# RWKV-7 chunk stage of a hybrid decoder step: the bonus products on GpSimd, the second half's new state, four filler matmuls and the first loads take other places

## The reference, cut to what matters

```python
def _wkv_step(S, inp):
    r, w, k, v, a, b = inp
    sa = jnp.einsum('bhvk,bhk->bhv', S, a)
    S = S * w[:, :, None, :] + sa[..., None] * b[:, :, None, :] + v[..., None] * k[:, :, None, :]
    return S, jnp.einsum('bhvk,bhk->bhv', S, r)
...
S_T, y = lax.scan(_wkv_step, wkv0, (tm(r), tm(decay), tm(k), tm(v), tm(-kk), tm(kk * a)))
mean = jnp.mean(y, axis=-1, keepdims=True)
var = jnp.mean(jnp.square(y - mean), axis=-1, keepdims=True)
y = ((y - mean) * lax.rsqrt(var + GN_EPS)).reshape(B, T, D) * ln_w + ln_b
y = y + (jnp.sum(r * k * r_k, axis=-1, keepdims=True) * v).reshape(B, T, D)
out = (y * g) @ w_o
```

## Time and profile before

| | us |
|---|---|
| median of 3 runs | 3388.64 |
| lowest and highest run | 3384.31, 3389.98 |
| the profiled execution's own time | 3387.22 |
| its span in the profile | 3385.5 |
| PE busy | 3241.1 (96%) |
| DVE busy | 1845.6 (55%) |
| ACT busy | 1334.3 (39%) |
| POOL busy | 1204.2 (36%) |

### The profile page before, as it was taken

How to read it: one execution, slowest core, us unless ns; L and a number is a source line. 1 busy time by engine, 2 the same in 40 slices (tenths; PEclk the granted TensorE clock), 3 DMA queues, 4 the chain that set the end, 5 groups by cost and what they waited for, 6 DMA issues and landing times.

```text
span 3385.5 us, 71725 instructions
## 1 busy us (share of the span) xinstructions
PE 3241.1 (96%) x26244; PEld 2942.4 (87%) x26244; DVE 1845.6 (55%) x3138; ACT 1334.3 (39%) x2785; POOL 1204.2 (36%) x842
## 2 busy tenths in 40 slices
PE   8999999999999999999999888988999999999998
PEld 6688887688999999989899777777887899999998
DVE  3566663126444588853332577677731644448885
ACT  2244445413545433313223445555421255543332
POOL 0000000012666777702232122222232076677771
PEclk9999999899999999999999899999969999999999
DMA  3122225401544544331232110001151054454442
GB/s 110 46 77 73 72 61 169 156 1 51 159 160 155 170 141 140 127 100 58 66 109 78 60 36 27 26 27 33 33 183 36 20 160 156 154 171 147 146 145 80
DMA packets 303577, 331.56 MB, mean 98 GB/s; under 512 B 54350, under 2 KB 285825, under 8 KB 303138
## 3 DMA queue, kind: packets, MB, share of 16 engines
q1 hardware_dynamic: 297346, 309.17, 28.6%
q0 software_dynamic: 6048, 19.73, 1.8%
HBM read 232.57 MB, written 116.69 MB: 103 GB/s over the span
## 4 chain that ended last, share of the span: by engine, by line
PE 74%; DVE 9%; PEld 6%; issue 4%; POOL 3%; ACT 2%; DMA 1%; SPq 1%; ACTq 1%; DVEq 0%; PEldq 0%; POOLq 0%
PE bank L631 70%; PEld bank L631 6%; PE bank L639 4%; POOL wloA L2034 1%; DVE arena L3547 1%; POOL arena L2034 1%; DVE arena L3701 1%; SPq L1662 1%; POOL wloS L2034 1%; DVE hT L3618 1%; DVE arena L3118 0%; ACT arena L2255 0%; ACTq L2714 0%; DVE arena L3010 0%; DVE arena L3564 0%
## 5 line engine op out<-in xcount | busy, mean ns | idle before, releaser
L631 PE MATMUL bank<-arena 128*128 128x268 f32 (+18 forms) x7294 | 972.7, 328 | 59.2 <-DVE hT L3618 15.5
L631 PEld LDWEIGHTS bank<-arena 128*128 128x128 f32 (+7 forms) x7294 | 756.5, 174 | 248.7 <-issue 43.1
L2255 ACT COPY arena<-bank 128x512 f32<-128x512 f32 (+15 forms) x523 | 233.4, 483 | 651.6 <-PE bank L631 450.6
L2034 POOL TENSOR_TENSOR arena<-arena 128x512 f32<-128x512 f32 x120 | 165.3, 1378 | 674.9 <-PE bank L631 448.3
L2478 ACT ACTIVATE whiS<-arena 128x512 fp32r<-128x512 f32 x180 | 113.0, 628 | 406.1 <-POOL arena L2034 392.9
L2034 POOL TENSOR_TENSOR wloA<-arena,whiA 128x512 fp32r<-128x512 f32 x180 | 261.6, 1468 | 0.4 <-ACT whiA L2475 0.4
L2034 POOL TENSOR_TENSOR wloS<-arena,whiS 128x512 fp32r<-128x512 f32 x180 | 238.8, 1341 | 49.1 <-ACT whiS L2478 49.1
L3413 DVE TENSOR_TENSOR hT<-hT,bank 128x536 f32<-128x536 f32 x280 | 197.6, 706 | 83.0 <-PE bank L631 82.6
L631 PE MATMUL bank<-hiT,whiS 128*128 128x268 f32 x768 | 199.9, 288 | 7.5 <-DVE loT L3255 3.8
L639 PE MATMUL bank<-table,arena 128*128 128x128 f32 (+5 forms) x1354 | 174.2, 271 | 31.2 <-DVE arena L3130 13.1
L3260 DVE TENSOR_TENSOR arena<-std,bank 128x268 f32<-128x268 f32 x192 | 80.4, 432 | 216.7 <-PE bank L631 208.4
(11 more groups left out here) (321 smaller groups left out, 8630.6 us busy)
## 6 DMA issues: line engine op xcount, KB each, us to landing
u_scratch<-arena SPq DMA_DIRECT2D x480, 134.0 KB, 1.8
arena<-in_ffn_w_up SPq DMA_DIRECT2D x64, 512.0 KB, 4.1
arena<-u_scratch SPq DMA_DIRECT2D x56, 536.0 KB, 5.2
arena<-in_ffn_w_down SPq DMA_DIRECT2D x112, 256.0 KB, 4.0
arena<-u_scratch SPq DMA_DIRECT2D x56, 402.0 KB, 6.0
arena<-past_scratch SPq DMA_DIRECT2D x32, 640.0 KB, 6.9
past_scratch<-in_cache_kv_latent SPq DMA_DIRECT2D x128, 128.0 KB, 2.4
past_scratch<-in_cache_k_rope SPq DMA_DIRECT2D x128, 32.0 KB, 2.1
```

Of the source, the lines that this page charges most:

```text
L631: return pe.matmul(out, lhsT, rhs, start=first, stop=last, skip_group_check=group)
L2034: return pool.tensor_tensor(out, a, b, op)
L2255: lane.do(act.copy(dst, b if view is None else view(b)), ring.drained)
```

## The change

It has four parts.

1. **GpSimd, `chunk`**: the bonus of a chunk is no longer the end of the chunk before. `bonus(c)` opens chunk c for c = 1 to 7, behind a wait for `low_b` (DVE has ended `low_inverses(c)`). The tail's bonus stays at the end of chunk 7. Since SyncE's load of r and k waits for the bonus, it moves too.
2. **DVE, `new_half`** is split. `new_taken` is the mask that frees the bank and stays; `new_summed` is the addition and the product. For the first half both follow each other as before. For the second half `new_summed(1)` moves behind `level_16(0)` of the next chunk, ahead of `scale_state`; in chunk 7 it stays.
3. **TensorE, `chunk`**: in chunk 0, which has no gates, four `keep_busy` matmuls stand where the others have the gates, behind `level_16(c, 1, ...)`.
4. **SyncE**: ahead of chunk 0 the load of r and k of chunk 1 comes first, ahead of the wait for the stores of v and the load of v of chunk 0.

```diff
@@ TensorE, chunk
                 if finish:
                     gates(c - 1, P)
+                else:
+                    for _ in range(4):
+                        keep_busy(ra)
@@ SyncE
+            bonus_b.wait(sp, 0)
+            load_r_k(1)
             for par in range(2):
                 sp.wait_ge(stg_s[par], staged_n)
             load_v(0, 0)
-            bonus_b.wait(sp, 0)
-            load_r_k(1)
             load_v(1, 1)
@@ GpSimd, chunk
+                if finish:
+                    low_b.wait(pool, c)
+                    bonus(c, P)
                 if prepare:
                     scale_keys(c + 1, wn)
...
                 if prepare:
                     decay_r(c + 1, 1 - par, wn)
+                if wn == TAIL:
                     bonus(c + 1, wn)
                 if finish:
                     store_z(c - 1)
@@ DVE
-            def new_half(d):
+            def new_taken():
                 b = ring.bank()
+                lane.do(dve.tensor_tensor(P1.rearrange("p (k w) -> p k w", k=4), b[:, :].rearrange("p (k w) -> p k w", k=4),
+                                          halves.unsqueeze(1).broadcast_to([P, 4, P]), ALU.mult), ring.drained)
+
+            def new_summed(d):
                 cts = slice(4 * d, 4 * d + 4)
                 new = P1.rearrange("p (k w) -> p k w", k=4)
-                lane.do(dve.tensor_tensor(new, b[:, :].rearrange("p (k w) -> p k w", k=4),
-                                          halves.unsqueeze(1).broadcast_to([P, 4, P]), ALU.mult), ring.drained)
                 lane.settle()
                 tt(new, new, Sm[:, cts, :], ALU.add)
                 lane.settle()
@@ DVE, chunk
                 level_16(0)
+                if finish:
+                    new_summed(1)
+                    lane.settle()
                 if isinstance(c, int) and c == 0:
                     dve.wait_ge(zero_s, 2)
                 scale_state()
...
-                new_half(0)
+                new_taken()
+                new_summed(0)
...
-                new_half(1)
+                new_taken()
+                if wn == TAIL:
+                    new_summed(1)
                 lane.settle()
```

## The result

| | before | after |
|---|---|---|
| median in the same comparison, us | 3389.31 (4 runs, 3384.31 to 3391.04) | 3355.45 (4 runs, 3353.59 to 3357.23) |
| profiled execution, its span, us | 3387.22, 3385.5 | 3356.99, 3355.3 |
| chunk stage, from its first product to the first of the tail's 256 products of 64x64: length, PEclk | 587.6 us (1873.06 to 2460.63), 0.94 | 552.4 us (1876.10 to 2428.45), 0.99 |

The ratio is 0.9902, with a 95% interval from 0.9885 to 0.992: 33.9 us faster. The forecast was 3356, 32.6 us.

What follows compares the result with a forecast made beforehand. TensorE, busy 96% of the time, bounds the kernel; only its idle or low-clock stretches count. Heads 20.3 + fillers 1.2 + earlier loads 11.1 = 32.6 us off 3387.2 gives 3354.6; median forecast 3356, range 3346 to 3375.

Steps and rivals of the forecast that it cites:

- the table: Gains up to each chunk head's first `level_32`; forecast 11.1 + 1.2 + 4.6 at chunk 1, then 4.6 or -1.35 each.
- The cause on DVE: At chunk heads: GpSimd's bonus slows `low_inverses`, 15.2 us against 12.1 without it, making L3764 late and TensorE wait 2.41.
- The masks are not slowed: At chunk heads: the moved bonus beside DVE's six masks costs 0; they take 3.79 us; the bound was 3 us.
- rival (b): Five heads give only 2 to 3 us each, say because GpSimd slows the masks; 3377 or 3366 us; chance 0.14.
- Part 2 "by itself worth about nothing": Second half's sums at chunk heads: 0.7 us gained ahead of the masks, 0.75 given back ahead of `blocks_32`.
- The five heads: Heads of chunks 1, 2, 4, 6 and 7, where TensorE waits for L3764: 4.6 us saved at each.
- The turns: Heads of chunks 3 and 5, where the loop turns: TensorE's 1.98 us "issue" idle stays fixed; 1.35 us lost each.
- rival (c): Loop turns were held by L3764 after all: two more heads at up to 3 us, 3347 us; chance 0.06.
- Part 3: Four fillers in chunk 0's 2.19 us gap keep TensorE's clock up: 1.2 us gained, bounds -0.3 and 1.5.
- Part 4: Earlier r and k in chunk 0: 3.5 gap gone, 2.0 lost to later stores, 9.6 from the clock; 11.1 us gained.
- rival (a): In chunk 0 the clock falls anyway, in gaps made by later stores of v: 3367 us; chance 0.24.
- rival (d): Later r and k make `scale_keys` miss ACT's squares by 3 us or more in six chunks: 3440 us; chance 0.05.

Runs made afterwards that it cites:

- the keys alone behind the wait: The changed kernel with the bonus back at the chunk's end and only `scale_keys` held behind `low_inverses`: 3361.98 us, ratio 0.992 to the kernel before.
- part 1 alone: The kernel before with only the bonus moved to open the chunk behind `low_inverses`: 3386.26 us, ratio 0.9994.
- part 4 alone: The kernel before with only r and k of chunk 1 loaded ahead of v of chunk 0: 3378.46 us, ratio 0.997.

## Why the prediction was right, and where it was not

The time is right to 0.6 us, and every step of the table to 1.4 us. That the total is so close is in part luck: the stage gained 2.6 us more than forecast, the profiled pair lost 5.0 at places that nobody edited, and one step of the reasoning, on part 2, was wrong. Point by point:

- **The cause on DVE** holds. `low_inverses` went from 15.2 to 11.8 us, near the 12.1 of chunk 0. But I named only the bonus, and L3764 was late for both pieces of GpSimd's work. The run with the keys alone behind the wait shows that `scale_keys` counts at least as much in time: without it 1.2 us less of DVE's work was enough to bring TensorE's wait from 2.41 to 1.21 us, where the clock stays.
- **The masks are not slowed** by the bonus: six took 3.80 us, 2.8 of them beside it. Here trace and forecast agree, and so does the rule quoted from the Trainium skill, GPSIMD Engine Reference, section 1: one operand of the masks is in PSUM. The upper bound of 3 us in rival (b) was not needed.
- **Part 2 "by itself worth about nothing" is the step that failed.** It rested on the sums ending at 2171.7, that is, on 1.42 us for them. But I had moved the bonus beside them two paragraphs earlier, and these are operations with two SBUF operands. At that place the run with part 1 alone has them at 4.72 us, and part 1 gains nothing without part 2. The section quoted names just this kind of operation; I applied it to the masks, found them free, and didn't apply it to the sums of the place before the move. The total came out right only because both parts were in the change. My factor for such sums was also too small: I had 2.79 for 1.42, and it is up to 3.3.
- **The five heads** gave 5.6, 5.1, 5.0 and 4.0 us for chunks 2, 4, 6 and 7, and about 5.8 for chunk 1, against 4.6. The mechanism is right, the size is 0.5 us short on average: at chunk 4 L3661 starts 8.3 us behind `b_with_r`'s start (2158.44 less 2150.15), where I had 8.7 by rounding each step of DVE up.
- **The turns** lost 1.2 and 1.5 us against 1.35. "Fixed" was right: rival (c) fell with the run that writes TensorE's loop out. What I had not seen is how much the turn costs as a whole, 6.8 us, since only 2 of it stand in one bracket.
- **Part 3**: 1.5 us in the trace for 1.2; the runs can't confirm it.
- **Part 4**: 10.95 us at the outputs of chunk 0 (1916.63 less 1873.06 before, 1908.72 less 1876.10 after) for 11.1. The stores of v landed 9.5 us after the stage's start instead of 6.9, 2.6 us later where I took 2 from bounds of 0 and 2.7; the gaps were 2.03 and 0.52 instead of 1.4 and 0.7. The clock held in after and fell in the run of part 4 alone, with a gap of the same length: rival (a) came nearer than its price suggests. Of the five traces with part 4 and such a gap (1.59 to 2.03 us) the clock fell in two, both at 1.96.
- **The load behind the bonus** (rival (d)): `scale_keys` started 5.06 us behind the bonus, as before (5.1), ended at 2161.07 and ACT's squares began at 2162.91, 1.8 us later. The slack I had worked out was 2.0.

## What to carry to other kernels

When two engines contend for SBUF, list for every place both what the moved work leaves and what it arrives beside, in the same units; a part of a change that looks idle may be what makes another part pay, so cost parts in both orders. A wait of an engine put down to "issue" where a loop turns is a price of that engine's own loop: writing the loop out for the one engine that bounds the kernel gained the whole price here, with the other engines' loops left as they were. And a gap of 2 us in front of a clocked engine should be priced with what the engine does behind it at the lower clock, not by its own length.

## What of the hardware was unexpected

- **VectorE beside GpSimd**: two sums of 128x512 with both operands in SBUF took 4.72 us beside GpSimd's 128x1024 products, 1.42 alone; each ended 0.5 us behind the end of the product that it began beside. That looks as if the sum waited for the product's end; this was not tested. A scalar_tensor_tensor of 128x256 took 2.09 for 0.48, and a tensor_scalar of 128x256, with one tensor operand, 0.99 for 0.35. Masks with an operand in PSUM took 0.63 each all the same, and GpSimd's own product only went from 1.91 to 2.24.
- **The turn of TensorE's loop** costs 6.8 us in the trace: two idle stretches of 1.76 and 2.28 us, and behind them products at a lower clock (24 of 64x128 in 4.64 us, 2.03 at chunk 4's head), which then make ACT late.
- **The clock** fell from 2.4 GHz to its lower level in gaps of 1.96 (in two runs), 2.41 and 3.55 us, and held in one of 2.03. Behind the gap of 3.55 it stayed at 0.50 for 22.56 us with TensorE busy all the time; behind the one of 1.96, where eight filler products followed, it was back when they had ended, 3.66 us later. What makes the difference was not told apart here.
- **Stores and loads at one time**: the stores of v, 1 MB, had landed (by the start of the load that waits for them) 6.9 us after the stage's start, 9.5 with 1 MB of loads started beside them, and 7.1 with the same loads started some 22 us earlier.
